# Loading the first three cached-key units into idle memory instead of the ring

## The chip, the cores and the metric

The kernel runs on one core of a Trainium2 chip. The metric is the device time of one execution in microseconds (us), as a median of several runs; lower is better.

## The reference

One inference step of a two-layer decoder for a prompt of 256 tokens and eight sampled sequences of 8 tokens each (320 rows of width 1024 in all). Layer 0 is half-FFN, mLSTM, half-FFN; then one shared K/V projection; layer 1 is half-FFN, attention, half-FFN; then a final RMSNorm. All weights and activations are float32. The part around the change is the attention of layer 1, where the eight sampled sequences also attend to 256 cached positions each, fetched through a page table:

```python
k_past = cache_k[page_table].reshape(bs, past_len, B_HEADS, B_HD)   # 8 sequences x 2 pages x 128 positions
v_past = cache_v[page_table].reshape(bs, past_len, B_HEADS, B_HD)
s = jnp.einsum('bqhd,bqhnkd->bqhnk', qf, kg.astype(F32)) * scale     # + ALiBi, mask, softmax
out = jnp.einsum('bqhnk,bqhnkd->bqhd', p, vg.astype(F32))
```

A page of keys or of values is 128 x 1024 floats, 512 KB. One sequence has two pages of keys and two of values.

## The kernel before

Weights are streamed in "units" of up to 1 MB through a ring `raw` of four slots. SyncE issues all of the loads in one fixed order and waits, ahead of each load, until the slot is free (`slot_free`): for a weight, until VectorE has made its low half (`lo_done`); for a cache unit, until TensorE has multiplied it (`kv_used`). ScalarE copies a weight unit to `w_hi` (rounded), VectorE subtracts to `w_lo`, and TensorE does three passes per product (L405 to L407).

The attention part stands between the query projection (four units, the last of them `U_Q + 3`) and the output projection (units from `U_OB`). In it 16 cache units are used: units 0 to 7 hold the keys of sequence 0 to 7, units 8 to 15 their values; each is two pages. In the ring they stand behind the first unit of the output projection (`U_OB`), so units 0 to 3 take the four slots before the attention begins and unit 4 needs the slot of unit 0. A unit's two loads are issued by `load_cache` (L381 reads the page number, L382 issues).

TensorE's order in the attention is written out by hand (L782 to L816): scores of prompt head 0; the scores of the new keys; cache units 0 and 1; then for each of eight prompt heads h: cache unit 2h+2, the transposes of head h's probabilities (`prompt_turn`, L698), the scores of head h+1 (L689, L690), cache unit 2h+3, the outputs of head h (L707, L708). Between a head's scores (L690) and its transposes (L698) lie VectorE's bias and maxima (L1541, L1545), ScalarE's exponentials (L1073), VectorE's reciprocal (L1550) and its scaling (L1552). For h = 1 and h = 3 VectorE and ScalarE also treat two groups of the samples' scores (`sample_bias` L1565, L1568; `sample_exp`), which TensorE transposes (`turn_probs`, L736 and L738) and VectorE spreads into the zeroed tile `p_spread` (`spread_probs`, L1575) before the samples' value products (L758) can start. TensorE multiplies a key unit in L727 and a value unit in L758.

GpSimd zeroes `q_spread`, `p_spread` and `p_new` (L1706 to L1708) once the units up to `U_Q` have been multiplied. These three tiles, with others of the attention, lie over the hidden activations of the FFN, which are dead by then. `work` is scratch; the attention uses its first 1536 columns.

Of the kernel before, what the change touches and what calls it, by code (L numbers as in the profile page):

```python
# [20 lines left out]
TP, NB, TS = 256, 8, 8  # L21
# [5 lines left out]
H = 8  # L27
DK, DV = 64, 128
HP = H // 2
PAST, PAGE = 256, 128  # L30
NPG = PAST // PAGE
# [4 lines left out]
RAW = 4  # L36
# [5 lines left out]
QB, SLOT, RB = 4, 32, 160  # L42
# [25 lines left out]
def trunk_program(nc, w_in, w_out, w_a, w_oa, w_kv, w_q, w_ob, w_gate, x_in, par_in, con_in, row_in,  # L68
                  c0_in, n0_in, kc_in, vc_in, pt_in,
                  y_out, k_out, v_out, cp_out, cs_out, np_out, ns_out, m_out):  # L70
    f32, f32r, i32 = mybir.dt.float32, mybir.dt.float32r, mybir.dt.int32
# [3 lines left out]
    with ctx:  # L75
        def sb(name, shape, dt=f32, where=ctx):
            return where.enter_context(nc.sbuf_tensor(name, shape, dt))

        def sem(name):
            return ctx.enter_context(nc.semaphore(name))  # L80

        raw = sb("raw", [128, RAW, PAIR])
# [11 lines left out]
        work = sb("work", [128, 10 * T])  # L94
# [10 lines left out]
        pages = sb("pages", [1, NB * NPG], i32)  # L105
# [3 lines left out]
        with ExitStack() as ov:  # L109
            with ExitStack() as own:  # L110

                qT = sb("qT", [128, HP, T], f32, own)
                kT = sb("kT", [128, HP, 384], f32, own)
                og = sb("og", [128, H, T], f32, own)
                kw = sb("kw", [128, 3, H * DK], f32, own)
                kwm = sb("kwm", [NS, 2, NB, DK], f32, own)
                rows = sb("rows", [128, T], f32, own)
                cols = sb("cols", [128, 3, 128], f32, own)
                g40 = sb("g40", [40, T], f32, own)
                fz = sb("fz", [8, T], f32, own)  # L120
                fa = sb("fa", [8, T], f32, own)
                cb = sb("cb", [8, T], f32, own)
                cm = sb("cm", [8, T], f32, own)
                neg = sb("neg", [8, 384], f32, own)
                mt = sb("mt", [8, T], f32, own)
                tmp = sb("tmp", [8, T], f32, own)
                mo = sb("mo", [8, 1 + NB], f32, own)
                dmat = sb("dmat", [128, 448], f32, own)
                pmat = sb("pmat", [128, 512], f32, own)
                qm = sb("qm", [128, 2, 4 * (NS + 2 * TS)], f32, own)  # L130
                c0 = sb("c0", [128, 2, 4, DV + 1], f32, own)
                cn = sb("cn", [128, 4, DV], f32, own)
                cpn = sb("cpn", [DK, DV], f32, own)
                ot = sb("ot", [128, 3, DV], f32, own)
                junk = sb("junk", [128, 3, DV], f32, own)
                ssqh, den, var, scl = (sb(n, [128, 3], f32, own) for n in ("ssqh", "den", "var", "scl"))
                ac_rhs = sb("ac_rhs", [8, 2, 4, H], f32, own)
                acb = sb("acb", [128, 4, H], f32, own)
                n0 = sb("n0", [NB, H, DK], f32, own)
                nn = sb("nn", [NB, H, DK], f32, own)  # L140
                al = sb("al", [NB, H], f32, own)
            k_all = sb("k_all", [128, H, T], f32, ov)
            with ExitStack() as own:
                f_hi = sb("f_hi", [128, FK, T], f32r, own)
                f_lo = sb("f_lo", [128, FK, T], f32r, own)
            with ExitStack() as own:
                qa = sb("qa", [128, H, T], f32, own)


                q_spread = sb("q_spread", [128, H, 2, RB], f32, own)  # L150
                p_spread = sb("p_spread", [128, NPG, 4, 4, RB], f32, own)
                p_new = sb("p_new", [128, 4, 128], f32, own)
                ss = sb("ss", [128, 4, PAST + SLOT], f32, own)
                o_rows = sb("o_rows", [128, 4, DV], f32, own)
                st = sb("st", [128, 2, 6], f32, own)
                sst = sb("sst", [128, 3, 4], f32, own)

        npp = pmat[0:1, :]
        ident, ones = con[:, C_ID:C_ID + 128], con[:, C_ONE:C_ONE + 128]
        sel = row[:, R_SEL:R_SEL + 1024].rearrange("k (h p) -> k h p", h=H)  # L160
        bank = [ctx.enter_context(nc.psum_tensor(f"bank{i}", [128, 512], f32)) for i in range(8)]
# [7 lines left out]
        loaded = [sem(f"raw_loaded{i}") for i in range(RAW)]  # L169
        hi_done = sem("weight_hi_done")  # L170
        lo_done = sem("weight_lo_done")
        unit_done = sem("unit_multiplied")
        kv_used = sem("cache_unit_used")
        pair_free = sem("pair_banks_evacuated")
        gate_ready = sem("gate_scaled")
        silu_ready = sem("silu_done")
# [17 lines left out]
        spread_set = sem("spread_zeros_set")  # L194
# [71 lines left out]
        at = 0  # L266
# [6 lines left out]
        U_Q = at; at += 4  # L273
        U_OB = at; at += 4
        U_FFN[3] = at; at += FFN_UNITS
        U_END = at
        CACHE = 2 * NB
        ORDER = (0, 2, 1, 3)


# [13 lines left out]

        def cached_at(r):

            return r - U_OB - 1 if U_OB < r <= U_OB + CACHE else None

        def unit_at(r):

            return r if r <= U_OB else r - CACHE

        def loads_after(r):

            return sum(16 if cached_at(q) is None else 16 * NPG for q in range(r % RAW, r + 1, RAW))

        def raw_of(n):

            return n if n <= U_OB else n + CACHE

        def raw_of_cache(c):

            return U_OB + 1 + c

        def width(n):
            return OUTU if any(f + FK <= n < f + FFN_UNITS for f in U_FFN) else PAIR
# [3 lines left out]
        def _(sp):  # L320
            def slot_free(r):

                before = r - RAW
                if before >= 0 and cached_at(before) is None:
                    sp.wait_ge(lo_done, unit_at(before) + 1)
                elif before >= 0:
                    sp.wait_ge(kv_used, cached_at(before) + 1)
# [43 lines left out]


            sp.wait_ge(s_pg, 16)
            def load_cache(c):

                r = raw_of_cache(c)
                src = kc_in if c < NB else vc_in
                slot_free(r)
                for j in range(NPG):
                    at = NPG * (c % NB) + j  # L380
                    page = sp.value_load(pages[0:1, at:at + 1], min_val=0, max_val=kc_in.shape[0] - 1)  # L381
                    sp.dma_start(raw[:, r % RAW, j * 1024:j * 1024 + 1024],  # L382
                                 src[bass.ds(page, 1), :, :].rearrange("a p c -> p (a c)")
                                 ).then_inc(loaded[r % RAW], 16)

            for c in range(CACHE):
                load_cache(c)
            for k in range(1, 4):
                load(raw_of(U_OB + k), w_ob[k], PAIR)
# [12 lines left out]
        def _(pe):  # L402
# [238 lines left out]
            for h in range(H):  # L641
# [4 lines left out]
                else:  # L646

                    pe.wait_ge(p_done, H)
                    for t in range(2):
                        pe.matmul(bank[4][0:1, :], ones[:, 0:1], kw[:, t, :], start=(t == 0), stop=(t == 1))  # L650
                    pe.matmul(bank[5][0:8, 0:8], con[0:64, C_LAST:C_LAST + 8], cols[0:64, 2, 64:72],
                              start=True, stop=True)
# [65 lines left out]

            def cache_scores(b):

                raw_at = raw_of_cache(b)
                pe.wait_ge(loaded[raw_at % RAW], loads_after(raw_at))
                keys = raw[:, raw_at % RAW, :].rearrange("p (g h k) -> p g h k", g=NPG, h=H)
                own = slice(SLOT * (b % 4), SLOT * (b % 4) + SLOT)
                for h in range(H):
                    k, out = h % QB, bank[2 * (h // QB) + b // 4]
                    mm = pe.matmul(out[SLOT * k:SLOT * k + SLOT, 0:PAST], q_spread[:, h, b // 4, own],  # L727
                                   keys[:, :, h, :], start=False, stop=(b % 4 == 3), skip_group_check=True)
                mm.then_inc(kv_used, 1)

            def turn_probs(i):
# [417 lines left out]
        def _(ve):  # L1149
# [377 lines left out]
            split_at(U_OB)  # L1527
            q_post(3)
            ve.wait_ge(pair_free, P_Q + 4)
            ve.wait_ge(spread_set, 3)  # L1530
            for q in range(2):
                ve.tensor_copy(q_spread[:, :, q, :].rearrange("p h (s x) -> p h s x", s=4)[:, :, :, 0:TS],
                               qa[:, :, TP + SLOT * q:TP + SLOT * q + SLOT].rearrange("p h (s t) -> p h s t", s=4)
# [36 lines left out]
            def spread_probs(i):  # L1570

                r = ORDER[i]
                ve.wait_ge(sm_t, i + 1)
                for pg in range(NPG):
                    ve.tensor_copy(p_spread[:, pg, r, :, :].rearrange("p k (s x) -> p k s x", s=4)[:, :, :, 0:TS],  # L1575
                                   bank[r][:, pg * 128:pg * 128 + 128].rearrange("p (k s t) -> p k s t", k=QB, s=4)
                                   ).then_inc(sm_tc, 1)
                own = slice(SLOT * (r % 2), SLOT * (r % 2) + SLOT)
                ve.tensor_copy(p_new[own, r, :], bank[r][own, 256:384]).then_inc(sm_tc, 1)
                ve.reciprocal(sst[:, 2, r:r + 1], sst[:, 1, r:r + 1]).then_inc(sm_r, 1)  # L1580
# [59 lines left out]
        def _(gp):  # L1640
# [63 lines left out]
            add_squares(4)  # L1704
            gp.wait_ge(unit_done, U_Q)
            gp.memset(q_spread[:, :, :, :], 0.0).then_inc(spread_set, 1)  # L1706
            gp.memset(p_spread[:, :, :, :, :], 0.0).then_inc(spread_set, 1)
            gp.memset(p_new[:, :, :], 0.0).then_inc(spread_set, 1)  # L1708
            add_squares(5)
            add_squares(6)  # L1710

# [119 lines left out]
```

## Time and profile before

| | us |
|---|---|
| median of 3 runs (1300.65 to 1302.66) | 1300.69 |
| the profiled execution's own time | 1301.33 |
| its span, first to last instruction | 1299.5 |
| TensorE busy | 1265.3 |
| VectorE busy | 735.6 |
| ScalarE busy | 582.1 |
| GpSimd busy | 102.8 |
| the attention part, from 981.2 to 1024.9 of the span | 43.7 |

The profile page gives shares for the whole span. For one stage, three other views are needed: the instructions in order of time, in which a bracket at the end of a line gives the idle time of the engine just before it and what ended it; the table by stretches of time, with each engine's busy time, TensorE's granted clock, the share of the DMA engines in use and what they moved; and the table of one line's or one tile's instructions, with the time of its DMAs from issue to landing.

### The profile page before, as it was taken

How to read it: one execution, taken by the hardware profiler on the slowest of the kernel's cores; microseconds unless marked ns; L12 is line 12 of the kernel's file. 1: busy time of each engine (PE TensorE's matmuls, PEld its weight loads, DVE VectorE, ACT ScalarE, POOL GpSimd, SP SyncE). 2: the span in 40 equal slices, each digit the busy share in tenths (PEclk: the TensorE clock that was granted, in tenths of full speed). 3: DMA queues.
4: the chain of work that ended last, by engine and by line, in shares of the span. 5: the costliest groups of instructions: out<-in, count | busy, mean ns of one | idle time of the engine just before them, and what ended most of it. 6: DMA issues, size and time to landing. Idle time of an engine off the chain costs nothing.

```text
span 1299.5 us, 21993 instructions
## 1 busy us (share of the span) xinstructions
PE 1265.3 (97%) x8841; PEld 1232.9 (95%) x8841; DVE 735.6 (57%) x1151; ACT 582.1 (45%) x922; POOL 102.8 (8%) x118
## 2 busy tenths in 40 slices
PE   6999999999999999999999999999998999999996
PEld 6999999999888999999999999999996899999996
DVE  7556554564666665554454555654555565655443
ACT  6445443453334555534343554533344364544332
POOL 2000000101333000000000000000020020000011
PEclk9999999999999999999999999999999999999998
DMA  8444344543224434434553644334458834343441
GB/s 297 162 140 151 121 134 148 196 133 127 89 92 140 151 138 161 142 99 156 168 180 135 220 156 157 134 110 148 163 179 299 329 123 163 137 161 108 133 147 40
DMA packets 36121, 200.52 MB, mean 154 GB/s; under 512 B 4426, under 2 KB 6602, under 8 KB 20570
## 3 DMA queue, kind: packets, MB, share of 16 engines
q1 hardware_dynamic: 33858, 192.37, 42.6%
q0 software_dynamic: 2208, 7.39, 1.7%
q8 instruction: 37, 0.61, 0.2%
q14 instruction: 18, 0.15, 0.0%
HBM read 193.17 MB, written 6.57 MB: 154 GB/s over the span
## 4 chain that ended last, share of the span: by engine, by line
PE 93%; DMA 2%; DVE 1%; issue 1%; ACT 1%; SPq 1%; POOL 0%; POOLq 0%; DVEq 0%; ACTq 0%
PE bank L405 29%; PE bank L407 29%; PE bank L406 29%; DMA raw<-vc_in 1%; PE bank L606 1%; PE bank L598 1%; DVE h_lo L1174 1%; PE bank L572 1%; DMA raw<-kc_in 0%; DMA raw<-w_in 0%; PE bank L573 0%; PE bank L521 0%; SPq L381 0%; PE bank L510 0%; ACT h_hi L865 0%
## 5 line engine op out<-in xcount | busy, mean ns | idle before, releaser
L405 PE MATMUL bank<-h_hi,w_hi 128*128 128x320 f32 x1920 | 598.0, 311 | 15.8 <-DVE h_lo L1174 14.2
L407 PE MATMUL bank<-h_hi,w_lo 128*128 128x320 f32 x1920 | 594.5, 310 | 0.0
L406 PE MATMUL bank<-h_lo,w_hi 128*128 128x320 f32 x1920 | 594.5, 310 | 0.0
L844 ACT ACTIVATE w_hi<-raw 128x1024 fp32r<-128x1024 f32 (+1 forms) x368 | 336.0, 960 | 461.0 <-PE bank L407 456.4
L1162 DVE TENSOR_TENSOR w_lo<-raw,w_hi 128x1024 fp32r<-128x1024 f32 (+1 forms) x368 | 393.1, 1109 | 116.4 <-ACT w_hi L844 116.1
L405 PEld LDWEIGHTS bank<-h_hi,w_hi 128*128 128x128 f32 x1920 | 361.7, 188 | 19.7 <-DVE w_lo L1162 12.0
L406 PEld LDWEIGHTS bank<-h_lo,w_hi 128*128 128x128 f32 x1920 | 361.7, 188 | 0.2
L407 PEld LDWEIGHTS bank<-h_hi,w_lo 128*128 128x128 f32 x1920 | 361.5, 188 | 0.0
L406 PE MATMUL bank<-f_lo,w_hi 128*128 128x320 f32 x704 | 217.5, 309 | 0.0
L407 PE MATMUL bank<-f_hi,w_lo 128*128 128x320 f32 x704 | 217.5, 309 | 0.0
L405 PE MATMUL bank<-f_hi,w_hi 128*128 128x320 f32 x704 | 217.4, 309 | 0.0
L405 PEld LDWEIGHTS bank<-f_hi,w_hi 128*128 128x128 f32 x704 | 132.2, 188 | 0.0
L407 PEld LDWEIGHTS bank<-f_hi,w_lo 128*128 128x128 f32 x704 | 132.2, 188 | 0.0
L406 PEld LDWEIGHTS bank<-f_lo,w_hi 128*128 128x128 f32 x704 | 132.2, 188 | 0.0
L1188 DVE TENSOR_TENSOR work<-bank,rms 128x320 f32<-128x320 f32 x88 | 43.2, 491 | 151.3 <-PE bank L407 150.8
L883 ACT ACTIVATE f_hi<-work 128x320 f32 (+1 forms) x88 | 41.6, 472 | 123.0 <-DVE work L1196 123.0
L1203 DVE TENSOR_TENSOR f_lo<-work,f_hi 128x320 f32 (+1 forms) x88 | 43.3, 492 | 66.2 <-ACT f_hi L883 66.2
L1652 POOL TENSOR_TENSOR sqsum<-sqsum,sq 128x320 f32<-128x320 f32 x49 | 52.1, 1064 | 276.6 <-ACT sq L862 274.5
L1649 POOL COPY sqsum<-sq 128x320 f32<-128x320 f32 x7 | 6.6, 942 | 724.0 <-ACT sq L862 723.9
L1208 DVE SCALAR_TENSOR_TENSOR x<-bank,x 128x320 f32<-128x320 f32 x32 | 15.7, 492 | 74.1 <-PE bank L407 74.1
L1174 DVE SCALAR_TENSOR_TENSOR h_lo<-x,par,h_hi 128x320 fp32r<-128x320 f32 x56 | 47.9, 892 | 13.0 <-ACT h_hi L865 13.0
L1196 DVE TENSOR_TENSOR work<-work 128x320 f32<-128x320 f32 x88 | 42.7, 486 | 6.6 <-ACT work L879 6.6
(195 smaller groups left out, 652.8 us busy)
## 6 DMA issues: line engine op xcount, KB each, us to landing
raw<-w_in SPq DMA_DIRECT2D x88, 1024.0 KB, 4.8
raw<-w_out SPq DMA_DIRECT2D x64, 704.0 KB, 4.1
raw<-w_a SPq DMA_DIRECT2D x12, 1024.0 KB, 4.8
raw<-w_kv SPq DMA_DIRECT2D x8, 1024.0 KB, 4.8
raw<-kc_in SPq DMA_DIRECT2D x16, 512.0 KB, 4.5
raw<-vc_in SPq DMA_DIRECT2D x16, 512.0 KB, 7.0
raw<-w_oa SPq DMA_DIRECT2D x4, 1024.0 KB, 5.9
raw<-w_q SPq DMA_DIRECT2D x4, 1024.0 KB, 4.8
```

What stands on the lines that cost most here:

```text
L405: pe.matmul(out, wh, mh, start=first, stop=False)
L406: pe.matmul(out, wh, ml, start=False, stop=False)
L407: return pe.matmul(out, wl, mh, start=False, stop=last)
L844: sc.activation(w_hi[:, n_at % 2, part * w:part * w + w], raw[:, raw_of(n_at) % RAW, part * w:part * w + w], ACT.Copy).then_inc(hi_done, 1)
L883: sc.activation(dst, up[:, k_at % 2, :], ACT.Copy).then_inc(hid_hi, 1)
L1162: ins = ve.tensor_tensor(w_lo[:, n_at % 2, c], raw[:, raw_of(n_at) % RAW, c], w_hi[:, n_at % 2, c].bitcast(f32), ALU.subtract)
L1174: ve.scalar_tensor_tensor(out=h_lo[:, m, :], in0=x[:, m, :], scalar=par[:, P_G + KT * norm + m:P_G + KT * norm + m + 1], in1=h_hi[:, m, :] ...
L1188: ve.tensor_tensor(gate[:, k_at % 2, :], bank[b][:, 0:T], rms[:, :], ALU.mult).then_inc(gate_ready, 1)
L1196: ve.tensor_tensor(up[:, k_at % 2, :], up[:, k_at % 2, :], act[:, k_at % 2, :], ALU.mult).then_inc(hid_ready, 1)
L1203: ve.tensor_tensor(lo, up[:, k_at % 2, :], hi.bitcast(f32), ALU.subtract).then_inc(hid_lo, 1)
L1208: ve.scalar_tensor_tensor(out=x[:, m, :], in0=bank[4 + m % 2][:, 0:T], scalar=0.5, in1=x[:, m, :], op0=ALU.mult, op1=ALU.add).then_inc(x_r ...
L1652: gp.tensor_tensor(sqsum[:, :], sqsum[:, :], sq[:, m % 2, :], ALU.add).then_inc(sum_done, 1)
```

## The change

Cache units 0, 1 and 2 no longer go through the ring. Their six pages are loaded into `p_spread` (units 0 and 1), into a new tile `page_k` and into columns 1536 to 2559 of `work` (unit 2). SyncE issues these six loads right behind that of `U_OB`, once the units ahead of `U_Q` have been multiplied. The ring's cache units are then 3 to 15: units 3 to 6 take the four slots ahead of the attention, and unit 7 needs the slot of unit 3.

Since a page of these units stands alone, their scores are made page by page: 16 products of 128 columns for each unit in place of 8 of 256 columns. GpSimd zeroes `p_spread` later, after cache unit 1 has been multiplied; VectorE waits for that ahead of its first `spread_probs`, and for two zeroed tiles in place of three ahead of spreading the queries.

```diff
+                page_k = sb("page_k", [128, 1024], f32, own)
...
+        spread_room = p_spread[:, :, :, :, :].rearrange("p a r k c -> p (a r k c)")
+        early_keys = [[spread_room[:, 0:1024], spread_room[:, 1024:2048]],
+                      [spread_room[:, 2048:3072], spread_room[:, 3072:4096]],
+                      [page_k[:, :], work[:, 1536:2560]]]
...
-        CACHE = 2 * NB
+        RING_CACHE = CACHE - EARLY
...
-            return r - U_OB - 1 if U_OB < r <= U_OB + CACHE else None
+            return r - U_OB - 1 + EARLY if U_OB < r <= U_OB + RING_CACHE else None
...
-            for c in range(CACHE):
+            sp.wait_ge(unit_done, U_Q)
+            for c in range(EARLY):
+                for j in range(NPG):
+                    sp.dma_start(early_keys[c][j], page_of(c, j)).then_inc(early_loaded[c], 16)
+            for c in range(EARLY, CACHE):
                 load_cache(c)
...
+                if b < EARLY:
+                    pe.wait_ge(early_loaded[b], 16 * NPG)
+                else:
+                    pe.wait_ge(loaded[raw_of_cache(b) % RAW], loads_after(raw_of_cache(b)))
                 own = slice(SLOT * (b % 4), SLOT * (b % 4) + SLOT)
-                for h in range(H):
-                    k, out = h % QB, bank[2 * (h // QB) + b // 4]
-                    mm = pe.matmul(out[SLOT * k:SLOT * k + SLOT, 0:PAST], q_spread[:, h, b // 4, own],
-                                   keys[:, :, h, :], start=False, stop=(b % 4 == 3), skip_group_check=True)
+                for g in range(2):
+                    out = bank[2 * g + b // 4]
+                    if b < EARLY:
+                        for j in range(NPG):
+                            for k in range(QB):
+                                c = (QB * g + k) * 128
+                                mm = pe.matmul(out[SLOT * k:SLOT * k + SLOT, j * PAGE:j * PAGE + PAGE],
+                                               q_spread[:, QB * g + k, b // 4, own], early_keys[b][j][:, c:c + 128],
+                                               start=False, stop=(b % 4 == 3), skip_group_check=True)
...
-            ve.wait_ge(spread_set, 3)
+            ve.wait_ge(spread_set, 2)
...
+                if i == 0:
+                    ve.wait_ge(spread_set, 3)
                 ve.wait_ge(sm_t, i + 1)
...
             gp.memset(q_spread[:, :, :, :], 0.0).then_inc(spread_set, 1)
+            gp.memset(p_new[:, :, :], 0.0).then_inc(spread_set, 1)
+            gp.wait_ge(kv_used, 2)
             gp.memset(p_spread[:, :, :, :, :], 0.0).then_inc(spread_set, 1)
-            gp.memset(p_new[:, :, :], 0.0).then_inc(spread_set, 1)
```

## Rows read from the trace of the kernel before

**Rows 1.** The page: the span, and the chain that ended last, by engine.

```profile
span 1299.5 us, 21993 instructions
PE 93%; DMA 2%; DVE 1%; issue 1%; ACT 1%; SPq 1%; POOL 0%; POOLq 0%; DVEq 0%; ACTq 0%
```

**Rows 2.** By stretches: length, PE, PEld, DVE, ACT, POOL busy, clock, DMA, GB/s.

```profile
975.00:980.00 5.00, 5.00 (x36) 5.00 (x35) 2.62 (x3) 2.72 (x3) 0.00 (x0) 1.00 0.23 81
...
985.00:990.00 5.00, 3.53 (x39) 1.90 (x27) 3.56 (x11) 2.03 (x7) 0.00 (x0) 1.00 0.80 256
...
1005.00:1010.00 5.00, 4.70 (x85) 3.51 (x80) 3.03 (x14) 1.86 (x6) 0.00 (x0) 1.00 1.03 410
...
1015.00:1020.00 5.00, 4.37 (x77) 3.27 (x77) 2.08 (x7) 2.13 (x7) 0.00 (x0) 1.00 1.04 418
```

**Rows 3.** Waits from 940 to 1040: total us, times, longest us.

```profile
PE bank L727 <- DMA raw<-kc_in: 3.0, 3, 1.8
PE bank L758 <- DMA raw<-vc_in: 2.5, 5, 0.8
```

**Rows 4.** TensorE in order of time in the attention: start, duration, line.

```profile
985.79 0.55 PE L698 MATMUL bank<-con,work 128*128 128x128 f32 x3 [0.32 <-DVE work L1552]
...
990.66 1.07 PE L727 MATMUL bank<-raw,q_spread 128*32 128x256 f32 x16 [1.81 <-DMA raw<-kc_in]
991.66 0.55 PE L698 MATMUL bank<-con,work 128*128 128x128 f32 x3
...
993.78 1.07 PE L727 MATMUL bank<-raw,q_spread 128*32 128x256 f32 x16 [0.92 <-DMA raw<-kc_in]
...
995.75 0.27 PE L738 MATMUL bank<-con,ss 128*32 128x128 f32 x1
...
997.70 0.49 PE L698 MATMUL bank<-con,work 128*128 128x128 f32 x3
...
1002.64 0.55 PE L698 MATMUL bank<-con,work 128*128 128x128 f32 x3
...
1004.53 1.08 PE L758 MATMUL bank<-raw,p_spread 128*32 128x128 f32 x32 [0.69 <-DMA raw<-vc_in]
...
1008.53 0.55 PE L698 MATMUL bank<-con,work 128*128 128x128 f32 x3
...
1013.20 0.55 PE L698 MATMUL bank<-con,work 128*128 128x128 f32 x3
...
1015.20 1.08 PE L758 MATMUL bank<-raw,p_spread 128*32 128x128 f32 x32 [0.80 <-DMA raw<-vc_in]
...
1017.76 1.08 PE L758 MATMUL bank<-raw,p_spread 128*32 128x128 f32 x32 [0.40 <-DMA raw<-vc_in]
1018.77 0.55 PE L698 MATMUL bank<-con,work 128*128 128x128 f32 x3
...
1023.07 0.55 PE L698 MATMUL bank<-con,work 128*128 128x128 f32 x3 [0.84 <-DVE work L1552]
```

**Rows 5.** VectorE in order of time: the reciprocals of heads 1, 2 and 7.

```profile
989.97 0.15 DVE L1550 RECIPROCAL st<-st 128x2 f32<-128x2 f32 x1
...
996.74 0.13 DVE L1550 RECIPROCAL st<-st 128x2 f32<-128x2 f32 x1
...
1022.26 0.17 DVE L1550 RECIPROCAL st<-st 128x2 f32<-128x2 f32 x1 [1.05 <-ACT work L1073]
```

**Rows 6.** Cache loads: issues of unit 4 and their landing; landing of all value pages.

```profile
L382 SPq DMA_DIRECT2D raw<-kc_in x2: 333/333/333, 984.5 to 985.6; - x2
DMA to landing us min/median/max: 3.4/4.2/4.9
...
DMA to landing us min/median/max: 6.5/7.0/7.8
```

**Rows 7.** GpSimd's zeroing of p_spread; VectorE's L1174 alone and beside GpSimd.

```profile
959.08 4.37 POOL L1707 MEMSET p_spread<- 128x5120 f32 x1
L1174 DVE SCALAR_TENSOR_TENSOR h_lo<-x,par,h_hi x39: 539/1162/1178, 181.0 to 945.5; 128x320 fp32r<-128x320 f32 x39
```

More of the change, by code:

```diff
@@ L173, in trunk_program @@
         kv_used = sem("cache_unit_used")
+        CACHE, EARLY = 2 * NB, 3
+        early_loaded = [sem(f"early_key_unit_loaded{i}") for i in range(EARLY)]
         pair_free = sem("pair_banks_evacuated")
@@ L295, in cached_at @@
         def cached_at(r):
-            return r - U_OB - 1 if U_OB < r <= U_OB + CACHE else None
+            return r - U_OB - 1 + EARLY if U_OB < r <= U_OB + RING_CACHE else None
         def unit_at(r):
-            return r if r <= U_OB else r - CACHE
+            return r if r <= U_OB else r - RING_CACHE
         def loads_after(r):
@@ L307, in raw_of @@
         def raw_of(n):
-            return n if n <= U_OB else n + CACHE
+            return n if n <= U_OB else n + RING_CACHE
         def raw_of_cache(c):
-            return U_OB + 1 + c
+            return U_OB + 1 + c - EARLY
         def width(n):
@@ L373, in _, with page_of @@
             sp.wait_ge(s_pg, 16)
+            def page_of(c, j):
+                at = NPG * (c % NB) + j
+                page = sp.value_load(pages[0:1, at:at + 1], min_val=0, max_val=kc_in.shape[0] - 1)
+                return (kc_in if c < NB else vc_in)[bass.ds(page, 1), :, :].rearrange("a p c -> p (a c)")
             def load_cache(c):
                 r = raw_of_cache(c)
-                src = kc_in if c < NB else vc_in
                 slot_free(r)
                 for j in range(NPG):
[L380 to L383, printed above, removed]
+                    sp.dma_start(raw[:, r % RAW, j * 1024:j * 1024 + 1024], page_of(c, j)
                                  ).then_inc(loaded[r % RAW], 16)
-            for c in range(CACHE):
+            sp.wait_ge(unit_done, U_Q)
[3 more added lines that the diff above has]
+            for c in range(EARLY, CACHE):
                 load_cache(c)
@@ L719, in cache_scores @@
             def cache_scores(b):
-                raw_at = raw_of_cache(b)
-                pe.wait_ge(loaded[raw_at % RAW], loads_after(raw_at))
-                keys = raw[:, raw_at % RAW, :].rearrange("p (g h k) -> p g h k", g=NPG, h=H)
+                if b < EARLY:
+                    pe.wait_ge(early_loaded[b], 16 * NPG)
+                else:
+                    pe.wait_ge(loaded[raw_of_cache(b) % RAW], loads_after(raw_of_cache(b)))
                 own = slice(SLOT * (b % 4), SLOT * (b % 4) + SLOT)
-                for h in range(H):
-                    k, out = h % QB, bank[2 * (h // QB) + b // 4]
-                    mm = pe.matmul(out[SLOT * k:SLOT * k + SLOT, 0:PAST], q_spread[:, h, b // 4, own],
-                                   keys[:, :, h, :], start=False, stop=(b % 4 == 3), skip_group_check=True)
+                for g in range(2):
[7 more added lines that the diff above has]
+                                               start=False, stop=(b % 4 == 3), skip_group_check=True)
+                    else:
+                        keys = raw[:, raw_of_cache(b) % RAW, :].rearrange("p (j h k) -> p j h k", j=NPG, h=H)
+                        for k in range(QB):
+                            mm = pe.matmul(out[SLOT * k:SLOT * k + SLOT, 0:PAST], q_spread[:, QB * g + k, b // 4, own],
+                                           keys[:, :, QB * g + k, :], start=False, stop=(b % 4 == 3),
+                                           skip_group_check=True)
                 mm.then_inc(kv_used, 1)
```

## The prediction, made before the changed kernel was run

> **What bounds the kernel now.** I read the page first: of the span of 1299.5 us, 93% of the chain that ended last is TensorE and 2% is DMA [rows 1]. The kernel as a whole is bound by TensorE, and a change to loads can win only where TensorE stands idle for them. So I went to the waits around the attention, the one stage in which cache pages are loaded. There TensorE stood idle for cache pages 3.0 us in 3 waits for keys and 2.5 us in 5 waits for values, 5.5 us in all [rows 3]. The table by stretches says why: from 995 on the DMA engines are busy all the time (share 1.03) at 410 to 418 GB/s, while from 975 to 980 they move 81 GB/s [rows 2]. A cache unit is 1.049 MB, so at 410 GB/s it takes 2.56 us, and the loop over prompt heads uses two units a pass, 5.1 us. The third thing to look at is how long a pass takes without loads. The marks of a pass are the transposes of a head's probabilities (L698). They start at 985.79, 991.66, 997.70, 1002.64, 1008.53, 1013.20, 1018.77 and 1023.07 [rows 4], so the passes took 5.87, 6.04, 4.94, 5.89, 4.67, 5.57 and 4.30 us, 37.28 in all. In the last one, where no further unit stands ahead of the transposes, the pass is the pure chain scores, bias, exponentials, reciprocal, scaling, transposes: 4.30 us. That chain is what is late next when the loads are not.
>
> **The change, part by part: what the ring does.** Before, units 0 to 3 are there when the attention starts; unit 4 is issued once unit 0 is multiplied, at 984.5 and 985.6 (two pages), and its last page landed 4.9 us after the second issue, at 990.5; TensorE began on it at 990.66 after 1.81 us of idling [rows 4, 6]. After, units 0 to 6 are there. Three units, 3.15 MB, leave the stretch in which the DMA engines are the limit for one in which they move 81 GB/s [rows 2]. Issued from about 953 at 1.1 us a page (the distance of unit 4's two issues [rows 6]), all six pages are on their way by 959.5 and down some 15 us before they are read; even at the 7.8 us of the slowest value page they'd be there by 968. The next ring slots come free only when the query units have been split, so behind these loads nothing that is waited for is delayed. I cost this at nothing; its cover is those 15 us.
>
> **Pass by pass, without the waits for pages.** A transpose follows its reciprocal by 1023.07 - 1022.26 = 0.81 us [rows 4, 5].
> - Pass 1 (to 991.66). VectorE's reciprocal of head 1 was at 989.97, before unit 4 was even multiplied, so without the wait the transposes start at 989.97 + 0.81 = 990.78: saves 0.88.
> - Pass 2 (to 997.70). Its reciprocal stands on VectorE behind the first spreading of the samples' probabilities, which needs TensorE's L738. From the transposes of head 1 to L738 went 995.75 - 991.66 = 4.09 us, of which 0.92 was the wait for unit 5 [rows 4] (the third wait for keys, 3.0 - 1.81 - 0.92 = 0.3 us for unit 6, came behind L738 and off this path), leaving 3.17; from L738 to the reciprocal 0.99; then 0.81. The pass takes 4.97 instead of 6.04: saves 1.07.
> - Pass 3 (4.94) had no wait for a page in it, and the pass 5 (4.67) neither: nothing.
> - Pass 4 (to 1008.53) is of the same build. The 0.69 for unit 9 stand ahead of its L738 [rows 4] and go: 5.20 instead of 5.89. The wait for unit 10 lay behind L738 and off the path.
> - Pass 6 (to 1018.77) held 0.80 for unit 13 and 0.40 for unit 14 [rows 4]: 5.57 - 1.20 = 4.37, just over the chain's 4.30: saves 1.20.
> - Pass 7 is the chain itself: TensorE idles 0.84 for the scaling right ahead of the transposes [rows 4], so what unit 15 waits doesn't count. Nothing.
>
> The sum is 0.88 + 1.07 + 0.69 + 1.20 = 3.84 us of the 5.5 that TensorE waited. The remaining 1.7 us is idle time that the softmax chain, not the pages, would take.
>
> **Do the pages arrive in time for that?** Unit 7 now waits for unit 3, used at about 988.0, so it is issued some 0.7 us after, at 988.7 and 989.8, and the DMA engines stand idle before. With 4.9 us [rows 6] it lands at 994.7; TensorE wants it near 996.9. From there on a unit is issued when the one four places before it is used, that is two passes earlier: 0.7 + 1.1 us until the second page is issued, the landing L, and 1.07 us to multiply it [rows 4]. With L = 7.0, the median of value pages, two passes can't be shorter than 9.9 us. The sums of two neighbouring passes above are 9.96, 9.91, 10.14, 9.87, 9.04 and 8.67. Only the last two are shorter, and by then units are ahead: counted from unit 6 (used from 994.0) unit 14 can start at 994.0 + 2 x 9.9 = 1013.8, where the sum wants it at about 1013.8; and unit 15, counted from unit 3 (986.9), at 1016.6 against 1016.0 wanted with 0.8 us of slack before the chain feels it. With L = 7.8 (the slowest) the same count gives unit 14 at 1015.4 and costs 1.6 us. So this term is 0 to 1.6 us. I take 0, since 7.0 and 7.8 were measured with the engines at 103% and six pages in flight [rows 2, 6], and the new stretch starts from empty queues.
>
> **The other edits.** The three early units are 32 weight passes of 128 columns instead of 16 of 256. A value unit has just that form and takes 1.08 us against a key unit's 1.07 [rows 4]: nothing. The bounds are 0 and the 0.3 us by which three units would touch the transposes of head 0 if each were a tenth slower.
> GpSimd now zeroes `p_spread` after unit 1, from about 984.8, taking 4.37 us [rows 7], so until 989.2. VectorE's new wait stands ahead of the first spreading, which by pass 2 above comes at about 994.3. It is covered by 5 us; behind it on VectorE would be head 2's reciprocal, and all further heads. GpSimd's next work, the squares after the output projection, is some 45 us off.
> But this zeroing now runs beside the softmax chain on VectorE. What two engines do to one another is seen in L1174, 539 ns at its quickest and 1162 at the median where GpSimd adds squares beside it [rows 7]: a factor of 2.16 at worst, 1.0 at best. Within 984.8 to 989.2 VectorE is busy about 3.3 us (3.56 in five [rows 2]). I take 0, because the zeroing reads nothing, and bound it at 3.3 x 1.16 = 3.8. The Trainium skill, GPSIMD Engine Reference, Key points, says that GpSimd shares its memory interfaces with VectorE and contends with instructions in a two-port mode or with two inputs in on-chip memory. By that rule only the scaling (L1552) of head 0, about 0.6 us, would be hit here, and the sum would be worse by at most 0.7 us. No row of this trace has the zeroing beside such a scaling.
>
> **After the attention.** The loads of the output projection keep their places behind units 12 to 15, so they come earlier with the rest. TensorE then works at full clock, and the waits for DMA of rows 3 are all that there are up to 1040, so the 3.84 us reach the end.
>
> **The sum.** The profiled execution has a span of 1299.5 and took 1301.33, 1.83 around it. 1299.5 - 3.8 = 1295.7, with what lies around it 1297.5. The median shown is 0.64 below that execution: 1296.9 us.
>
> **The rivals.**
> 1. *The pages stay the limit* (L near 7.8 us): four slots turn round too slowly, costing 1.6 us as above. For it: DMA at 103% and a demand of two units a pass, 5.1 us, while the new passes are mostly shorter. Against it: three units fewer to move. Time 1298.5.
> 2. *The chain is quicker than the old passes show*: spreading comes between only because TensorE's L738 was late; then passes 2 and 4 go down to 4.30, another 0.67 + 0.90 = 1.6 us. For it: nothing else on VectorE is in the way. Against: my count of L738 has no wait in it any more. Time 1295.3.
> 3. *Slower: the zeroing and VectorE hold each other up.* Place: GpSimd's L1707 beside the chain, from 984.8. With the factor 2.16 the zeroing would last 9.4 us, until 994.2. VectorE is busy 735.6 of 1299.5 us, 0.57, so it has some 5.3 us of work in that time, longer by 5.3 x 1.16 = 6.2; net 2.4 us slower, 1303.1. It decides from a factor of 1.7 up (5.3 x 0.7 = 3.7, which eats the gain). Against it: the factor comes from an addition that reads two tiles, the zeroing only writes.
> 4. *The gain is lost later or the loads don't come early*: 1300.7. Against it: no wait for a load between 1024.9 and 1040 in the view of rows 3, and 15 us of cover.
>
> **How the numbers follow.** Forecast 1296.9 with 0.70; rival 1 0.15, of which a third still counts as faster; rival 2 0.07; rival 3 0.04; rival 4 0.04. A change of 0.2%, 2.6 us, is about what a measurement of this kernel can tell from none, so faster starts below 1298.1. Faster: 0.70 + 0.05 + 0.07 = 0.82; same: 0.10 + 0.04 = 0.14; slower 0.04. The range reaches from rival 2 to just past rival 1: 1295.3 to 1298.8.
>
> **What the profile of the changed kernel would show.** Right: transposes (L698's successor) at about 985.8, 990.8, 995.8, 1000.7, 1005.9, 1010.6, 1014.9 and 1019.2; no wait for pages of units 4 to 6; waits for pages below 1.5 us in all; DMA at a low rate from 984 to 988.7; the zeroing 4.4 us long and done before 990; VectorE's bias and maxima of head 1 as long as those of head 7. Wrong: waits of TensorE for units 10 to 15 over 1.5 us together (rival 1), a zeroing of 9 us or a doubled bias (rival 3), or the first transposes later than 985.8, which would mean that the early units or the memory they stand in cost something that I put at nothing.

## The result, and the profile after

The changed kernel took 1303.82 us (median of 19 runs, 1302.01 to 1305.17) against 1300.91 for the kernel before, measured beside it. The medians lie 2.9 us apart; the ratio, 1.0017 with a 95% interval of 1.0011 to 1.0024, makes it 2.2 us slower (1.4 to 3.1). I had forecast 3.8 us less. Its profiled execution took 1304.27 us with a span of 1302.5.

The first view is again TensorE in order of time (start, duration, line, idle time before it and what ended it). L711 are now the transposes of a head's probabilities, L745 and L751 the products with early and with ring key units, L720 and L721 the outputs of a prompt head, L783 those with value units.

```profile
982.33 0.38 PE L702 MATMUL bank<-k_all,qa 128*128 128x128 f32 x2
...
986.23 0.40 PE L745 MATMUL bank<-work,q_spread 128*32 128x128 f32 x8
990.48 0.55 PE L711 MATMUL bank<-con,work 128*128 128x128 f32 x3 [3.85 <-DVE work L1577]
...
991.61 1.91 PE L751 MATMUL bank<-raw,q_spread 128*32 128x256 f32 x16
993.45 1.22 PE L720 MATMUL bank<-work,v_tok 128*128 128x256 f32 x2
...
996.20 0.55 PE L711 MATMUL bank<-con,work 128*128 128x128 f32 x3
...
1001.13 0.55 PE L711 MATMUL bank<-con,work 128*128 128x128 f32 x3
...
1006.11 0.55 PE L711 MATMUL bank<-con,work 128*128 128x128 f32 x3 [0.47 <-DVE work L1577]
...
1011.24 0.55 PE L711 MATMUL bank<-con,work 128*128 128x128 f32 x3 [0.25 <-DVE work L1577]
...
1015.71 0.55 PE L711 MATMUL bank<-con,work 128*128 128x128 f32 x3
...
1020.07 1.08 PE L783 MATMUL bank<-raw,p_spread 128*32 128x128 f32 x32 [0.79 <-DMA raw<-vc_in]
1021.08 0.55 PE L711 MATMUL bank<-con,work 128*128 128x128 f32 x3
...
1025.38 0.55 PE L711 MATMUL bank<-con,work 128*128 128x128 f32 x3 [0.84 <-DVE work L1577]
...
1027.19 0.39 PE L418 MATMUL bank<-h_hi,w_hi 128*128 128x320 f32 x1
```

Where the kernel before went from its first scores (981.21) to the output projection (1024.87) in 43.66 us, this one takes 1027.19 - 982.33 = 44.86. The waits for unit 4 and for unit 5 [rows 4] are gone, as forecast. In their place stands one wait of 3.85 us ahead of head 0's transposes, where there had been 0.32 [rows 4]. What ends it is VectorE's L1577, the scaling of head 0's probabilities. VectorE and, below it, GpSimd in the same stretch:

```profile
986.11 0.17 DVE L1575 RECIPROCAL st<-st 128x2 f32<-128x2 f32 x1 [1.05 <-ACT work L1098]
986.31 4.12 DVE L1577 TENSOR_SCALAR work<-work,st 128x128 f32<-128x128 f32 x2
991.72 0.55 DVE L1566 SCALAR_TENSOR_TENSOR work<-con,bank 128x384 f32<-128x384 f32 x1 [1.29 <-PE bank L703]
...
985.85 4.37 POOL L1736 MEMSET p_spread<- 128x5120 f32 x1 [25.13 <-PE bank L745]
```

Two instructions that take 0.55 us elsewhere take 4.12 here. They start 0.46 us into the zeroing of `p_spread`. The zeroing ends at 990.22, the first of the two (3.98 us long) 0.07 us behind it and the second, at 990.43, 0.2 us behind it. The zeroing itself is as long as before, 4.37 us [rows 7].

Two more things hang on this. The table by stretches (length; busy time of TensorE's products, of its weight loads, of VectorE, ScalarE and GpSimd; TensorE's clock; DMA share; GB/s) shows both:

```profile
980.00:985.00 5.00, 4.67 (x97) 4.27 (x100) 2.40 (x7) 0.00 (x0) 0.00 (x0) 1.00 0.66 214
985.00:990.00 5.00, 1.63 (x60) 1.36 (x52) 3.91 (x4) 0.98 (x4) 4.15 (x1) 1.00 0.00 1
990.00:995.00 5.00, 4.52 (x27) 2.58 (x27) 2.97 (x8) 1.86 (x6) 0.21 (x1) 0.67 0.00 0
995.00:1000.00 5.00, 4.91 (x59) 2.86 (x62) 2.97 (x10) 2.88 (x11) 0.00 (x0) 0.99 0.85 297
```

TensorE was busy 1.63 of 5 us, and right behind that its granted clock is 0.67 on the mean of 5 us: it fell from 2.4 to 1.2 GHz for part of them. Unit 3 took 1.91 us instead of 1.07 [rows 4]. And the DMA engines moved next to nothing from 985 to 995 (0 to 1 GB/s): the seven units that fit are there, and unit 7 may start only when unit 3 has been multiplied, at 993.5 instead of the 988.0 of the forecast.

### The profile page after: what moved, and what is told of

The parts are those of the page before. It is cut to its first block, busy times and chain, and to the rows that moved or that the text cites. A ratio compares the mean times of both kernels' runs of the same rounds, so it can differ in the third digit from the quotient of the medians.

```text
span 1302.5 us, 22095 instructions
## 1 busy us (share of the span) xinstructions
PE 1269.1 (97%) x8889; PEld 1237.0 (95%) x8889; DVE 739.3 (57%) x1151; ACT 581.7 (45%) x922; POOL 102.8 (8%) x118
## 4 chain that ended last, share of the span: by engine, by line
PE 95%; DVE 2%; issue 1%; DMA 1%; ACT 1%; SPq 0%; POOL 0%; POOLq 0%; DVEq 0%; ACTq 0%
PE bank L418 30%; PE bank L419 29%; PE bank L420 29%; PE bank L619 1%; PE bank L611 1%; DMA raw<-vc_in 1%; PE bank L585 1%; DVE work L1577 0%; PE bank L586 0%; DMA raw<-w_in 0%; PE bank L475 0%; PE bank L534 0%; PE bank L523 0%; PE bank L615 0%; PE bank L631 0%
```

## The experiments

All are measured against the kernel before, which was run anew beside them (medians 1301.5, and 1302.26 for the last three: zeroing shorter, zeroing behind the scaling again, two-input form timed), so the ratios say more than the times; "attention" is the stretch of TensorE's time from the first scores to the first product of the output projection (43.66 before, 44.86 changed).

**Without the late zeroing.** This kernel leaves out the zeroing of the 4096 columns that held keys, so its samples' values are not the reference's.

```diff
-            gp.wait_ge(kv_used, 2)
-            gp.memset(p_spread[:, :, :, :, :], 0.0).then_inc(spread_set, 1)
+            gp.memset(spread_room[:, 4096:5120], 0.0).then_inc(spread_set, 1)
```

> The changed kernel without the late zeroing of p_spread (only its last 1024 columns are zeroed, early; so the samples' value products work on key data in the unused columns and their result isn't the reference's). Theory A (the zeroing on GpSimd holds VectorE's scaling of head 0, and all of the loss follows from that): the scaling of 128 and 256 columns takes 0.55 us together instead of 4.12, TensorE's idle time ahead of head 0's transposes is 0.3 us instead of 3.85, the clock stays at its upper level in the attention, and from the first scores to the output projection go 39.8 us (43.7 before, 44.9 in the changed kernel); time 1297 to 1298.5. Theory B (the early units or where they lie cost TensorE something, or the pages come no earlier): at least 43 us for the attention and a time of 1300 or more.

Measured: 1297.59 us, ratio 0.9969 (0.9958 to 0.9981), attention 1021.15 - 980.77 = 40.38 us. Head 0's scaling and what TensorE waits for:

```profile
984.75 0.55 DVE L1577 TENSOR_SCALAR work<-work,st 128x128 f32<-128x128 f32 x2
...
985.35 0.55 PE L711 MATMUL bank<-con,work 128*128 128x128 f32 x3 [0.29 <-DVE work L1577]
...
990.33 0.55 PE L711 MATMUL bank<-con,work 128*128 128x128 f32 x3 [0.92 <-DVE work L1577]
...
1009.95 0.55 PE L711 MATMUL bank<-con,work 128*128 128x128 f32 x3
...
1011.49 1.08 PE L783 MATMUL bank<-raw,p_spread 128*32 128x128 f32 x32 [0.34 <-DMA raw<-vc_in]
...
1014.03 1.08 PE L783 MATMUL bank<-raw,p_spread 128*32 128x128 f32 x32 [0.39 <-DMA raw<-vc_in]
1015.04 0.55 PE L711 MATMUL bank<-con,work 128*128 128x128 f32 x3
```

Theory A holds. From the first scores to head 0's transposes go 4.58 us, as in the kernel before (8.15 in the changed one): the early units, their narrower products and their place cost nothing that shows there, and the 4.48 us that the changed kernel needs more than this one for the attention come with the zeroing.

**The late zeroing alone, in the kernel before**

```diff
             gp.memset(q_spread[:, :, :, :], 0.0).then_inc(spread_set, 1)
-            gp.memset(p_spread[:, :, :, :, :], 0.0).then_inc(spread_set, 1)
             gp.memset(p_new[:, :, :], 0.0).then_inc(spread_set, 1)
+            gp.wait_ge(kv_used, 2)
+            gp.memset(p_spread[:, :, :, :, :], 0.0).then_inc(spread_set, 1)
...
+                if i == 0:
+                    ve.wait_ge(spread_set, 3)
```

> The kernel before with one edit: p_spread is zeroed after cache unit 1, as in the changed kernel; no early units. Theory A: the same 4 us hold of head 0's scaling, 3.8 us of idling and a drop of the clock; while TensorE stands still the pages of units 4 and 5 land, so their waits (1.81 and 0.92) vanish and it loses less than it stalls: attention 45.5 to 47 us, time 1303 to 1305.5. Theory B (the hold comes from the loads into p_spread or from reading keys there, not from the zeroing): scaling 0.55 us and the time as before, 1300.9.

Measured: 1303.43 us, ratio 1.0013 (1.0004 to 1.0022), attention 1028.52 - 982.81 = 45.71 us. No key is loaded into `p_spread` here, and the hold is the same:

```profile
986.79 4.09 DVE L1552 TENSOR_SCALAR work<-work,st 128x128 f32<-128x128 f32 x2
...
986.31 4.36 POOL L1711 MEMSET p_spread<- 128x5120 f32 x1 [25.11 <-PE bank L727]
...
990.94 0.90 PE L698 MATMUL bank<-con,work 128*128 128x128 f32 x3 [3.86 <-DVE work L1552]
```

**The zeroing in 16 pieces**

```diff
-            gp.memset(p_spread[:, :, :, :, :], 0.0).then_inc(spread_set, 1)
+            for piece in range(16):
+                ins = gp.memset(spread_room[:, 320 * piece:320 * piece + 320], 0.0)
+            ins.then_inc(spread_set, 1)
```

> The changed kernel with the late zeroing cut into 16 pieces of 320 columns, issued one behind the other. If VectorE's scaling is held for as long as one GpSimd instruction lasts (theory A1), each of its two parts waits for at most one piece, about 0.3 to 0.6 us: scaling 1 to 1.7 us in all, time 1298 to 1300. If GpSimd keeps the shared access as long as it has work (A2), the scaling takes as long as all the pieces, 4 us or more, and the time is 1303 or more.

Measured: 1297.72 us, ratio 0.9964 (0.9951 to 0.9977), attention 40.52 us.

```profile
986.78 0.74 DVE L1577 TENSOR_SCALAR work<-work,st 128x128 f32<-128x128 f32 x2
...
986.32 5.18 POOL L1737 MEMSET p_spread<- 128x320 f32 x16 [25.12 <-PE bank L745]
```

A1: the scaling loses 0.19 us, less than I gave it (the time, too, is just below my range), and the sixteen pieces take 5.18 us instead of 4.37, which nobody waits for. The hold doesn't last for as long as GpSimd has work; it ends with the instruction that is running.

**The zeroing shorter** tells the same from the other side. This kernel leaves 2048 columns with keys in them, so its samples' values are not the reference's either.

```diff
+            gp.memset(spread_room[:, 4096:5120], 0.0)
             gp.wait_ge(kv_used, 2)
-            gp.memset(p_spread[:, :, :, :, :], 0.0).then_inc(spread_set, 1)
+            gp.memset(spread_room[:, 0:2048], 0.0).then_inc(spread_set, 1)
```

> The changed kernel with a late zeroing of 2048 columns instead of 5120 (the last 1024 are zeroed early, those of unit 1's keys are left, so the samples' values aren't the reference's). If the scaling is held exactly until the end of the one zeroing instruction: zeroing 1.75 us, held some 1.3 us instead of 3.6 (scaling 1.4 to 1.6 us), TensorE's idling ahead of head 0's transposes 1.1 to 1.3 us, clock stays up, attention 41 to 41.8 us, time 1298 to 1299.5. If the hold is a fixed price of about 3.6 us: attention near 44.9 us and 1303.

Measured: 1300.33 us, ratio 0.9985 (0.9975 to 0.9994), attention 1021.97 - 980.72 = 41.25 us.

```profile
984.70 1.55 DVE L1577 TENSOR_SCALAR work<-work,st 128x128 f32<-128x128 f32 x2
...
984.24 1.80 POOL L1737 MEMSET p_spread<- 128x2048 f32 x1 [24.24 <-PE bank L745]
...
986.31 0.55 PE L711 MATMUL bank<-con,work 128*128 128x128 f32 x3 [1.29 <-DVE work L1577]
```

The scaling ends 0.21 us after the zeroing (984.24 + 1.80 = 986.04; 986.25), as in the changed kernel. The clock stayed up: pass 1 took 991.28 - 986.31 = 4.97 us. The time came out 0.8 us above the range I had given, with the kernel before at 1302.26 beside it; the stretch lies within its range.

**The zeroing behind head 0's scaling**

```diff
+            gp.memset(spread_room[:, 4096:5120], 0.0)
             gp.wait_ge(kv_used, 2)
-            gp.memset(p_spread[:, :, :, :, :], 0.0).then_inc(spread_set, 1)
+            gp.wait_ge(pr_p, 1)
+            gp.memset(spread_room[:, 0:4096], 0.0).then_inc(spread_set, 1)
```

> The changed kernel, but the late zeroing waits for head 0's scaling too, and covers only the 4096 columns that held keys (the other 1024 are zeroed early). It then runs from about 985.9 to 989.4 beside the bias and the maxima of head 1 and is over before the scaling of head 1 at 990.2. Theory A with the hold on VectorE's scaling only (one input and output, both in on-chip memory): bias 0.55 and maxima 0.61 us as ever, attention 39.8 to 40.3 us, time 1297 to 1298.5. If the zeroing holds every VectorE instruction: the bias or maxima of head 1 last until 989.4, attention 42 us or more, time 1299.5 or more.

> The late zeroing behind head 0's scaling, once more and beside the two-input form on the same chip. Both should lie within 0.1% of one another, 1297 to 1299, and the stretch from the first scores to the output projection at 40.0 to 40.3 us. If the first measured median of 1299.2 was the kernel's own and not a matter of how often the clock falls ahead of the attention, this one is again over 1 us slower than the other.

Measured: 1299.24 us with ratio 0.9972 (0.9961 to 0.9984) at first and 1298.4 us with 0.9973 (0.9963 to 0.9984) the second time; attention 39.96 and 40.42 us. From the first:

```profile
988.57 0.55 DVE L1566 SCALAR_TENSOR_TENSOR work<-con,bank 128x384 f32<-128x384 f32 x1 [1.30 <-PE bank L703]
989.15 0.61 DVE L1570 TENSOR_REDUCE st<-work 128x1 f32<-128x128 f32 x2
...
991.69 0.55 DVE L1577 TENSOR_SCALAR work<-work,st 128x128 f32<-128x128 f32 x2
...
987.38 3.52 POOL L1738 MEMSET p_spread<- 128x4096 f32 x1 [25.37 <-DVE work L1577]
```

The first time lies 0.7 us above its range; the second, with the kernel of the two-input form at 1298.71 beside it, is not slower than that one, so by the test set down beforehand the 1299.24 was not the kernel's own. The bias (one operand in PSUM, the memory that TensorE writes to) and the maxima run inside the zeroing at their usual length. So of the forms that fell into the zeroing only the scaling's is held, and the zeroing is free if it falls between two scalings.

**Another form, or another engine, for head 0's scaling**, with the zeroing left where it was.

```diff
                 for i, c in enumerate((slice(0, 128), slice(128, 384))):
+                    if h == 0:
+                        ins = ve.tensor_tensor(pp[:, 0, c], pp[:, 0, c],
+                                               st[:, 0, 4 + i:5 + i].to_broadcast([128, 256 if i else 128]), ALU.mult)
+                        continue
                     ins = ve.tensor_scalar(pp[:, h % 2, c], pp[:, h % 2, c], st[:, h % 2, 4 + i:5 + i], None,
                                            ALU.mult)
```

> The changed kernel with VectorE scaling head 0 by a product of two tensors in on-chip memory (the second is the inverse sum, repeated) in place of the form with a scalar. In the kernel before, the making of low weight halves, which also reads two tensors there, started 0.4 us before the end of the zeroing and wasn't longer. If a two-input form runs beside the zeroing: 0.4 to 0.8 us for the two parts, attention 40.3 to 41 us. If it is held as well: 4 us, attention 44 to 45 us.

> The changed kernel with head 0 scaled by the two-input form, timed. Attention 40.3 us as in the first look; time 1297 to 1298.5, faster than the kernel before by 0.2 to 0.35%.

Measured: attention 40.30 us in a first, single execution (1296.28 us) and 40.45 in the same kernel timed ten times, which took 1298.71 us, ratio 0.9976 (0.9967 to 0.9986), where I expected at most 1298.5. From the first:

```profile
983.52 0.63 DVE L1578 TENSOR_TENSOR work<-work,st 128x128 f32<-128x128 f32 x2
...
983.05 4.37 POOL L1740 MEMSET p_spread<- 128x5120 f32 x1 [25.13 <-PE bank L745]
```

The two-input form starts at the same point of the same zeroing and is not held. Its 0.63 us beside the zeroing are a little more than the 0.55 us of the held form alone, and 3.5 us less than the 4.12 of that form beside the zeroing.

> The changed kernel with the late zeroing left as it is, 5120 columns at once behind cache unit 1, but the scaling of head 0 done by ScalarE. If only that one form of VectorE's instruction is held (one tensor read and one written, both in on-chip memory, times a scalar), nothing is held now: VectorE's bias and maxima of head 1 take 0.55 and 0.61 us, the zeroing 4.37 us beside them, ScalarE needs some 0.3 us more than VectorE for the scaling, the attention lasts 40.3 to 40.9 us and the time is 1297.5 to 1299.5. If the zeroing holds more of VectorE's work: bias or maxima of head 1 end only with the zeroing, attention over 42 us.

That variant has ScalarE do head 0's scaling (`sc.activation(..., ACT.Copy, scale=...)`). Measured: 1298.04 us, ratio 0.9979 (0.9970 to 0.9989), attention 1021.60 - 980.96 = 40.64 us, zeroing 4.37 us. It takes 0.80 us on ScalarE. The same result by a third way.

**TensorE kept at work during the hold**

```diff
+                if h == 0:
+                    for _ in range(24):
+                        pe.matmul(bank[7][:, 0:T], w_hi[:, 0, 0:128], h_hi[:, 0, :], start=True, stop=True)
                 prompt_turn(h)
```

> The changed kernel with 24 products of 320 columns into a bank that isn't in use, ahead of head 0's transposes: they fill 3.5 of the 3.85 us in which TensorE waits for the held scaling. If the lower clock behind that wait (unit 3 in 1.91 us instead of 1.07) comes from TensorE's idling, it stays at the upper level, and pass 1 is shorter by 0.8 to 1.3 us: attention 43.4 to 44 us against 44.9, time 1302 to 1303.2. If the clock falls for another reason: as the changed kernel, 44.9 us and 1303.8.

Measured: 1302.49 us, ratio 1.0006 (0.9997 to 1.0015), attention 1025.53 - 981.08 = 44.45 us.

```profile
985.31 3.79 PE L832 MATMUL bank<-h_hi,w_hi 128*128 128x320 f32 x24
989.24 0.55 PE L711 MATMUL bank<-con,work 128*128 128x128 f32 x3
...
990.38 1.07 PE L751 MATMUL bank<-raw,q_spread 128*32 128x256 f32 x16
...
994.21 0.55 PE L711 MATMUL bank<-con,work 128*128 128x128 f32 x3 [0.91 <-DVE work L1580]
...
1018.41 1.08 PE L783 MATMUL bank<-raw,p_spread 128*32 128x128 f32 x32 [1.04 <-DMA raw<-vc_in]
```

The clock stays at its upper level (unit 3 in 1.07 us, pass 1 in 4.97 instead of 5.72), so its fall came from TensorE's idling. But of these 0.75 us only 0.4 reach the end of the attention, less than expected: TensorE now waits 1.04 us for unit 14, where the changed kernel waited 0.79 and the one without the late zeroing 0.39. That the ring of loads stood still during the hold doesn't explain it: the second page of unit 14 was issued 21.49 us after head 0's transposes here and in the kernel without the late zeroing alike. It landed 7.6 us after its issue here and 7.1 there. Why it took longer is open.

**One early unit, none of it in `p_spread`**

```diff
-        CACHE, EARLY = 2 * NB, 3
+        CACHE, EARLY = 2 * NB, 1
...
+        early_keys = [[page_k[:, :], work[:, 1536:2560]]]
...
-            gp.wait_ge(kv_used, 2)
```

> Only one unit is loaded early, into page_k and work; p_spread holds no keys and is zeroed where it was in the kernel before. No hold. One unit of 1.05 MB less (2.6 us) in the stretch where the DMA engines are the limit: pass 1 takes 5.0 us instead of 5.87, waits for value pages remain at about 2 us, the attention lasts 41 to 41.8 us, time 1298 to 1299.5. If all of the gain of three early units came already with the first (the other two gain nothing), the attention lasts 40.0 to 40.5 us.

Measured: 1299.47 us, ratio 0.9988 (0.9979 to 0.9997), attention 1021.17 - 979.27 = 41.90 us; TensorE waited 2.6 us for value pages in 7 waits and 0.6 for one key unit:

```profile
PE bank L781 <- DMA raw<-vc_in: 2.6, 7, 0.6
...
PE bank L749 <- DMA raw<-kc_in: 0.6, 1, 0.6
```

The stretch ended 0.1 us above my range. One early unit gives 1.76 us of it, three give 3.28 (without the hold), so the first brings more than its share; two were not tried.

## Why the prediction was wrong, point by point

- **What bounds the stage** was right: pages for TensorE, and behind them the softmax chain.
- **The sum over the passes** was right but for one term. Without the zeroing the passes take 4.98, 4.94, 4.97, 5.13, 4.58, 5.09 and 4.31 us; I had 4.99, 4.97, 4.94, 5.20, 4.67, 4.37 and 4.30. Pass 6 is 0.72 off, the 0.34 and 0.39 us for units 13 and 14 in the rows above. This is the term of the pages' arrival, for which I took 0 of 0 to 1.6 us; it measured 0.7. The stretch got 3.28 us shorter instead of 3.84, and the time of that kernel, 1297.59, lies 0.7 us from my figure. The sum wanted unit 14 1013.8 - 985.8 = 28.0 us after head 0's transposes, and it started after 1014.03 - 985.35 = 28.68; its second page took 7.1 us to land, which is about the 7.0 that I had counted with, so empty queues at the start of the stretch were no help to it.
- **The step that failed** is "I take 0, because the zeroing reads nothing". I had asked by what factor VectorE's work would be longer, took the factor 2.16 from L1174, a two-input form beside an addition [rows 7], and spread it over all of VectorE's work. What happens is something else: one form, the product with a scalar where input and output are in on-chip memory, isn't done until GpSimd's zeroing is over; the others that fell beside it aren't touched. The same two instructions went from 0.55 to 4.12 us, a factor of 7.5. I had named the right place and time, had even seen which instruction would be hit, and had priced the collision as a ratio of durations where it is the rest of the other engine's instruction: 985.85 + 4.37 - 986.31 = 3.9 us. My upper bound of 3.8 us for this term happens to cover the 3.57 measured, but it was worked out from the wrong mechanism, and neither the forecast nor the range (to 1298.8) had any of it.
- **The row that I misread.** The trace of the kernel before had what looks like a hold in it, in the very instructions from which I took the factor:

```profile
180.91 0.48 POOL L1649 COPY sqsum<-sq 128x320 f32<-128x320 f32 x1 [162.91 <-ACT sq L862]
181.00 0.74 DVE L1174 SCALAR_TENSOR_TENSOR h_lo<-x,par,h_hi 128x320 fp32r<-128x320 f32 x1
...
955.67 1.30 POOL L1652 TENSOR_TENSOR sqsum<-sqsum,sq 128x320 f32<-128x320 f32 x1 [9.32 <-ACT sq L862]
...
956.14 1.17 DVE L1174 SCALAR_TENSOR_TENSOR h_lo<-x,par,h_hi 128x320 fp32r<-128x320 f32 x1
```

  L1174 ends 0.35 us after GpSimd's copy (181.39; 181.74) and 0.34 us after its addition (956.97; 957.31). A fixed factor would have made both equally long; a hold to the end of GpSimd's instruction gives 0.74 and 1.17. No experiment varied this pair, so the hold is read from its rows, not shown by an edit.
- **The page of the Trainium skill** that I weighed (GPSIMD Engine Reference, Key points) names two kinds of instructions that contend: two-port forms and those with two inputs in on-chip memory. The traces agree for the first, if the scaling is of it. For the second they agree beside a copy or an addition of GpSimd's, which read memory (L1174 above), and differ beside the zeroing, which only writes: the two-input scaling took 0.63 us there. That the contention is a hold to the end of an instruction isn't said in that section; from "contends" I had made "at most 0.7 us".
- **Rival 3** had the mechanism's place, but not its form, and 0.04 of chance. It spoke of a zeroing of 9.4 us and of all VectorE work; the zeroing stayed at 4.37. That its time, 1303.1, lies so near to the 1303.82 measured is luck. Nor did the sign for it appear, a zeroing of 9 us or a doubled bias. The sign that did, the first transposes later than 985.8 (they came at 990.48), I had tied to the early units and their memory, which cost nothing.
- **From the hold to the result.** Against the kernel without the late zeroing the stretch is 4.48 us longer: 3.57 until head 0's transposes (8.15 against 4.58 from the first scores), 0.74 in pass 1 (5.72 against 4.98), which is the lower clock, and 0.28 in pass 6, the pages, of which it isn't shown that they come from the hold; pass 5 gives 0.11 back. Against the kernel before this leaves 4.48 - 3.28 = 1.20 us.
- **The remaining 1.8 us between the two profiled executions** (spans 1302.5 and 1299.5). Of these 1.12 lie ahead of the attention, which starts at 982.33 instead of 981.21. In layer 0, where both kernels are the same, the clock falls at times: in the stretches 330 to 360 and 360 to 390 it was 1.00 and 0.94 before, and in the changed kernel

```profile
330.00:360.00 30.00, 30.00 (x183) 25.66 (x181) 18.39 (x57) 11.78 (x39) 11.55 (x15) 0.94 0.27 89
360.00:390.00 30.00, 30.00 (x186) 25.89 (x185) 18.06 (x56) 11.66 (x39) 9.72 (x13) 0.94 0.28 91
```

  In all profiled executions of this study the attention starts between 979.3 and 983.1: at 979.3 and 979.5 in the two where this clock never fell, from 980.7 to 981.2 with one fall, from 982.3 to 983.1 with two. So that part goes with the clock of layer 0, not with the change. The other 0.68 us lie behind the attention (275.31 us to the end of the span, against 274.63); with the same change and the same hold the kernel with filled idle time needs 274.67 there, so they aren't a fixed price of the change, and their cause is open. This scatter of several us is why single times here say less than the stretch in the trace.
- **From the stretch to the medians.** The ratio says 2.2 us (1.4 to 3.1), the stretch of one execution 1.20. Part of the rest seems to be a lower clock that lasts longer in other executions. Over the 19 runs of the changed kernel the granted clock was 0.9924 on the mean, against 0.9946 to 0.9950 for the kernel before beside the experiments; the difference of 0.0022 or more is that of some 6 us (0.0022 x 1302 x 2 = 5.7) at the lower level, an estimate from these means, where the profiled execution has 3.4 us of it in the attention. The kernel before with its zeroing moved had it for longer in its trace, at 0.50 from 990 to 995 and at 0.89 from 995 to 1000, and 45.71 us. And with TensorE kept at work the mean is 0.9947 and the ratio 1.0006, some 1.4 us less than the changed kernel's, of which the stretch shows 0.4. These means count the falls in layer 0 too, so this is argued, not shown stretch by stretch.

## What to carry to other kernels

When an edit moves GpSimd work in time, list VectorE's instructions that fall beside it by form, and price a collision of a zeroing with a float32 product with a scalar within on-chip memory as a hold for what remains of the GpSimd instruction, not as a slow-down. Beside GpSimd instructions that read memory, price two-input forms the same way until a run says otherwise. And before you take a ratio of durations from a group of rows, lay the start and end of single rows beside those of the other engine. Cut such work into small instructions, put it behind the critical instruction, or give that instruction another form or another engine: each of these brought the attention to 40.0 to 40.6 us and made the kernel 0.2 to 0.4% faster than before, where the change as made is slower. A stall of this length has a second price, the lower clock behind it: 0.74 us of the stretch here.

## What the hardware showed that I had not expected

- A zeroing of 5120 columns on GpSimd (4.37 us) holds a TENSOR_SCALAR of VectorE for 3.6 us, one of 2048 columns (1.80 us) for 1.0; with sixteen pieces of 320 columns the loss is 0.19 us. The one zeroing isn't lengthened by it.
- A TENSOR_TENSOR with both inputs in on-chip memory isn't held by it (0.63 us for 384 columns). A SCALAR_TENSOR_TENSOR beside a copy or an addition of GpSimd's ended 0.34 to 0.35 us after that instruction (L1174 in the kernel before).
- A wait of TensorE of 3.85 us was followed by the lower clock; waits of 1.81 [rows 4] and 1.29 us weren't, and neither was the same stretch filled with products.
